# Moving two of the delta rule's four output gate units from the inverses to the input products

## The chip, the cores and the metric

The kernel runs on one core of one Trainium2 chip. The metric is device microseconds of one execution, from the first to the last instruction of the program with what the runtime puts around them. The kernel before takes 2339.52 us, the median of three runs (2337.86, 2339.52 and 2339.65).

## What is computed

A trunk of two layers over 512 latent tokens and 256 context tokens, model width 1024. Each layer mixes the tokens by three groups of heads (gated DeltaNet, latent attention, HGRN2) that share one input and one output projection, and then runs a squared ReLU MLP. The part that matters here, cut from the reference:

```python
def gdn_mixer(pc, px, conv_w, a_log, dt_bias, norm_g, want_ctx):
    # pc, px: columns of h @ w_in for context and latent tokens
    # 0..2: q, k, v (512 columns each)   3: output gate (512 columns)   4, 5: beta and decay
    ...
    def readout(o, gate):
        b, l = gate.shape[:2]
        y = rms_norm(o, norm_g) * jax.nn.silu(gate.astype(F32).reshape(b, l, GDN_HEADS, GDN_DV))
        return y.reshape(b, l, GDN_HEADS * GDN_DV).astype(gate.dtype)
```

Inside `gdn_scan`, each chunk of 64 tokens needs the inverse of a unit lower triangular 64x64 matrix (`triangular_solve` of `eye + lower`). The gate isn't used before the readout, behind the scan. In the last layer the context gets no output, so its gate is not needed.

## The kernel before

**Layout.** Activations lie transposed: 8 blocks of 128 features, 768 tokens along the free axis (256 context, then 512 latent). `lo` is 0 in the first layer and 256 in the second, whose outputs are wanted for latent tokens alone. A unit is 128 output columns of a weight matrix, so `qkv` has 12 units and `gate` 4. A load is 256 columns of weights (1 MB), two units. Loads go through a ring of three slots of the tile `weights`, in the order of the list `LOADS`; SyncE issues a load when the unit that used the slot's last content (`weights_used`) is out. `UNITS` is the order in which units take the four pairs of PSUM banks, and the order of the counter `gemm_evac`.

**Input products.** `qkv` and `ba` units are products in fp32r of high and low parts: ScalarE copies the weights rounded to fp32r (`proj_high_part`, L1747), VectorE subtracts to get the rest (`proj_low_part`, L2300), and TensorE forms high x high, low x high and high x low for each of 8 blocks (`products`, L871, called by `gemm_parts`; `gemm_context_last`, L931, in the second layer). ScalarE then pads each unit (L1894, L1895), VectorE convolves it with five taps (L2430 to L2434) and ScalarE applies Silu (L1902, L1903). Between units 7 and 8 comes a small transpose (`bat`); the decays' chain (L2447 to L2454) follows unit 8 and releases `la_ready`, for which TensorE waits behind unit 9.

**The inverses.** They run over sizes 2, 4, 8, 16 and 32 with two halves `t` of three chunks each. Per size and half TensorE does a first product of 48 small fp32 matmuls (L1180), VectorE masks it (L2534), TensorE does a second product (L1192), and VectorE transposes it (L2550) and adds it to both sides (L2552, L2555), which releases the next size's first product by `u_ready`. The last size (L1177, L1189 to L1195) is handed on by copies of ScalarE (L2015), VectorE (L2546) and GpSimd (L781). GpSimd multiplies decays and attention meanwhile (L770 to L776), once a broadcast of the decays has come back from memory. Behind the last size, products of constants keep TensorE at work (L849), then the corners follow.

**The gates.** The four gate units are spread over the inverses as plain fp32 products, one block of 128 features at a time (`gate_products`: L1151 for 256 context columns, first layer alone, L1152 for 512 latent ones). `gate_work(p)` issues the steps of slot `p` behind each product, by the hand-written table `step_ends`; the first entry is done ahead of the first size. All four units use the same banks 6 and 7, so a unit's first step waits for ScalarE to have emptied the unit before (`hold_gate`, L2000 and L2001), which applies Silu and sends the gate to memory; it comes back much later. Each gate buffer is a half of `state` (`gate_stage`).

## Time and profile before

| | |
|---|---|
| median of 3 runs | 2339.52 us (2337.86 to 2339.65) |
| the profiled execution | 2341.05 us, span 2339.0 us |
| mean granted TensorE clock | 0.988 |
| TensorE busy | 2251.5 us, 96% of the span |
| VectorE, ScalarE, GpSimd busy | 1186.0, 872.9 and 226.6 us |
| input products of the delta rule, first layer | about 58 to 170 us |
| its inverses, first layer | 214 to 294 us |
| input products, second layer | about 1355 to 1458 us |
| its inverses, second layer | 1490 to 1560 us |

Times within the execution are microseconds from the start of the span. PE is TensorE, DVE VectorE, ACT ScalarE, POOL GpSimd and SP SyncE. Rows of the chain of waits give start, length and the piece of work; a plain fp32 matmul of the program appears there as two records (x2), an fp32r one as one. Rows of the timeline merge equal neighbours (xN), so the first start and the length of the merged row count; the shape is that of the first record. A row's length includes the drain, so the spacing of starts tells the rate.

### The profile page before, as it was taken

Reading aid. Unit: us, or ns where it says so; the run is one execution under the profiler, and the core shown is the slowest. Engines: PE = TensorE matmul, PEld = TensorE weight load, DVE = VectorE, ACT = ScalarE, POOL = GpSimd, SP = SyncE. Lnnn points to the kernel's source line nnn. Section 1 sums busy time; section 2 is a strip of 40 time slices with the busy share of each in tenths; the row PEclk is TensorE's granted clock in tenths of the full one; section 3 lists DMA queues with packets and bytes.
Section 4 is the critical chain, followed back from the end, with each engine's and each line's share of the span. In section 5 each row is a group of like instructions: output and inputs, shape, how many; then the busy total and the mean of one; then the engine's idle time right before and its main releaser. Section 6 shows DMA issues by size and latency. Waiting matters only on the chain.

```text
span 2339.0 us, 40119 instructions
## 1 busy us (share of the span) xinstructions
PE 2251.5 (96%) x17754; PEld 1833.2 (78%) x17754; DVE 1186.0 (51%) x1886; ACT 872.9 (37%) x1276; POOL 226.6 (10%) x226
## 2 busy tenths in 40 slices
PE   7999999999999999999999999999998999999998
PEld 5876698876668788888888687668885669888887
DVE  3685353287363651424333497546258556444444
ACT  5363134125463421212123546332324555232233
POOL 3013410000030100000000021511000121000000
PEclk9999999999999999999999999999998999999999
DMA  9218101134211121212121131411116301333222
GB/s 320 63 55 277 45 19 60 54 110 142 87 34 37 37 90 55 72 55 72 55 73 54 54 117 51 135 52 37 54 55 213 119 19 55 108 96 102 90 90 72
DMA packets 161684, 198.27 MB, mean 85 GB/s; under 512 B 18359, under 2 KB 129433, under 8 KB 160872
## 3 DMA queue, kind: packets, MB, share of 16 engines
q1 hardware_dynamic: 155536, 185.24, 24.3%
q10 hardware_dynamic: 5271, 10.10, 1.3%
q8 instruction: 140, 2.29, 0.4%
q0 software_dynamic: 704, 0.37, 0.2%
q14 instruction: 33, 0.26, 0.0%
HBM read 184.64 MB, written 11.06 MB: 84 GB/s over the span
## 4 chain that ended last, share of the span: by engine, by line
PE 86%; DVE 6%; ACT 4%; issue 2%; DMA 1%; POOL 0%; DVEq 0%; ACTq 0%
PE ps L1625 35%; PE ps L871 14%; PE ps L1543 5%; PE ps L1152 3%; PE ps L1021 2%; PE ps L962 2%; PE ps L1478 2%; PE ps L1582 2%; PE ps L1297 1%; PE ps L1315 1%; PE ps L858 1%; PE ps L1180 1%; PE ps L1491 1%; DVE region L2432 1%; PE ps L1192 1%
## 5 line engine op out<-in xcount | busy, mean ns | idle before, releaser
L1625 PE MATMUL ps<-region_r 128*128 128x512 f32 (+1 forms) x1536 | 376.8, 354 | 0.0
L1625 PEld LDWEIGHTS ps<-region_r 128*128 128x128 f32 x1536 | 270.3, 188 | 40.8
L1625 PE MATMUL ps<-region_r,weights_r 128*128 128x512 f32 (+1 forms) x768 | 229.6, 353 | 0.0
L2293 DVE TENSOR_TENSOR weights_r<-weights,region_r 128x2048 fp32r<-128x2048 f32 x62 | 141.9, 2289 | 119.1 <-ACT region_r L1761 119.0
L1625 PE MATMUL ps<-mixed_r,weights_r 128*128 128x512 f32 (+1 forms) x672 | 200.9, 353 | 0.0
L1625 PE MATMUL ps<-modulated_r,region_r 128*128 128x256 f32 (+1 forms) x624 | 186.7, 354 | 0.0
L1625 PE MATMUL ps<-mixed_r,region_r 128*128 128x256 f32 (+1 forms) x624 | 186.6, 353 | 0.0
L2222 ACT ACTIVATE region<-ps,cst 128x768 f32<-128x768 f32 (+1 forms) x64 | 50.4, 798 | 301.2 <-PE ps L1625 282.9
L1625 PEld LDWEIGHTS ps<-region_r,weights_r 128*128 128x128 f32 x768 | 144.3, 188 | 20.5
L2821 DVE TENSOR_TENSOR region_r<-region 128x768 fp32r<-128x768 f32 (+1 forms) x64 | 52.8, 825 | 202.2 <-ACT region L2222 202.2
L1625 PEld LDWEIGHTS ps<-mixed_r,weights_r 128*128 128x128 f32 x672 | 126.3, 188 | 18.1
L1625 PEld LDWEIGHTS ps<-modulated_r,region_r 128*128 128x128 f32 x624 | 117.2, 188 | 16.6
L1625 PEld LDWEIGHTS ps<-mixed_r,region_r 128*128 128x128 f32 x624 | 117.3, 188 | 16.5
L1761 ACT ACTIVATE region_r<-weights 128x2048 fp32r<-128x2048 f32 x62 | 118.4, 1910 | 10.6 <-DMA weights<-in_w_mlp 10.6
L871 PE MATMUL ps<-residual_r,weights_r 128*128 128x512 f32 (+1 forms) x432 | 117.4, 344 | 0.0
L2228 ACT ACTIVATE region<-ps 128x768 f32<-128x768 f32 (+1 forms) x48 | 33.9, 707 | 216.3 <-PE ps L1625 216.3
L2828 DVE TENSOR_TENSOR region<-region 128x768 f32<-128x768 f32 (+1 forms) x32 | 26.4, 826 | 138.9 <-ACT region L2228 138.9
L871 PEld LDWEIGHTS ps<-residual_r,weights_r 128*128 128x128 f32 x432 | 81.1, 188 | 10.6 <-issue 0.2
L739 POOL CAST region_r<-modulated 128x768 fp32r<-128x768 f32 (+2 forms) x24 | 26.1, 1130 | 583.8 <-ACT modulated L1830 546.7
L2300 DVE TENSOR_TENSOR weights_r<-weights,state_r 128x2048 fp32r<-128x2048 f32 x14 | 32.1, 2292 | 84.4 <-ACT state_r L1747 84.4
L1152 PE MATMUL ps<-modulated,weights 128*128 128x512 f32 x128 | 68.9, 636 | 5.2 <-issue 4.4
L871 PE MATMUL ps<-region_r,weights_r 128*128 128x256 f32 (+1 forms) x288 | 73.4, 337 | 0.0
(460 smaller groups left out, 4882.8 us busy)
## 6 DMA issues: line engine op xcount, KB each, us to landing
weights<-in_w_mlp SPq DMA_DIRECT2D x64, 1024.0 KB, 5.3
weights<-in_w_ada SPq DMA_DIRECT2D x40, 1024.0 KB, 5.3
weights<-in_w_in SPq DMA_DIRECT2D x34, 1024.0 KB, 5.3
region<-in_w_ada SPq DMA_DIRECT2D x8, 1024.0 KB, 16.6
weights<-in_w_out SPq DMA_DIRECT2D x8, 1024.0 KB, 6.6
x_kept<-residual SPq DMA_DIRECT2D x2, 3072.0 KB, 12.4
region<-decays_kept ACTq DMA_DIRECT2D x4, 1536.0 KB, 11.0
residual<-x_kept SPq DMA_DIRECT2D x2, 3072.0 KB, 9.9
```

The source lines that it names most:

```text
L871: last = mm(dst[:, CTX + a:CTX + b], w[:, k, m], r[k][:, a:b], start=(k == 0 and w is high and r is r_high), stop=(k == KB - 1 and r is r_ ...
L962: last = mm(dst[:, CTX + a:CTX + b], mat, sq[:, a:b], start=(k == 0), stop=(k == n - 1))
L1021: last = mm(ps[32 * k:32 * k + 32, bank, :], cs[:, 4 * half + k, :], w[:, k, :], start=(half == 0), stop=(half == 1))
L1152: last = mm(ps[:, 6, :], w, Hm[:, k, CTX:TOK], start=(k == 0), stop=(k == KB - 1))
L1478: last = mm(dst[:, CTX + s0:CTX + s1], QH[0:96, h, 128 * qt:128 * qt + 128], KH[0:96, h, s0:s1], start=True, stop=True)
L1543: last = mm(dst[:, at:at + b - a], w[:, k, m], r[:, a:b], start=(k == 0 and part_of == "low"), stop=(k == 5 and w is low))
L1582: last = mm(o, w[:, k, m], r[:, k, a:b], start=(k == 0 and r is Hm_r), stop=(k == KB - 1 and w is low))
L1625: last = mm(dst[:, CTX + a:CTX + b], w[:, k, m], r[:, a:b], start=(k == 0 and r is r_low), stop=(k == KB - 1 and w is low))
L1761: af(mlp_high(j), ring[:, n % NSLOT, :], ACT.Copy).then_inc(w_high_ready, 1)
L2222: copied(l, what, u, af(hid[:, b, lo:], src, ACT.Relu, bias=zero_col))
L2293: v.tensor_tensor(ring_r[:, at, :], ring[:, at, :], mlp_high(j), ALU.subtract).then_inc(w_low_ready, 1)
L2821: v.tensor_tensor(hid_high[:, b, lo:], z, z, ALU.mult)
```

## The change

Units 0 and 1 of the gate leave the inverses. They become fp32r products of high and low parts like `qkv`'s, computed between `bat` and `qkv` unit 8 (`early_gates`). Their weights' load moves from behind the `ada` loads to between `qkv` 3 and `qkv` 4; ScalarE makes the high part in `region` area 5 (`early_gate_high`) and VectorE the low part in the ring. ScalarE's and VectorE's parts of `qkv` 4 and 5 are made later than before. Their Silu goes to block 7 of `residual`, one after the other, and from there to memory (`hold_early_gate`); GpSimd waits for these stores before it clears `residual`. Units 2 and 3 stay as they are, with `step_ends` about halved.

```diff
-    LOADS += [(_l, "qkv", _i) for _i in range(3)] + [(_l, "ba", 0)] + [(_l, "qkv", _i) for _i in range(3, 6)]
+    LOADS += [(_l, "qkv", _i) for _i in range(3)] + [(_l, "ba", 0), (_l, "qkv", 3), (_l, "gate", 0), (_l, "qkv", 4), (_l, "qkv", 5)]
     LOADS += [(_l, "ada", ADA_GDN_AT[_l] + _i) for _i in range(2 * ADA_GDN[_l])]
-    LOADS += [(_l, "gate", _i) for _i in range(2)] + [(_l, "hq", _i) for _i in range(2)] + [(_l, "hf", _i) for _i in range(4)]
+    LOADS += [(_l, "gate", 1)] + [(_l, "hq", _i) for _i in range(2)] + [(_l, "hf", _i) for _i in range(4)]
...
-UNITS = ([("norm0", 0)] + [("qkv", i) for i in range(6)] + [("ba", 0), ("qkv", 6), ("qkv", 7), ("bat", 0), ("qkv", 8), ("qkv", 9), ("gcum", 0)]
+UNITS = ([("norm0", 0)] + [("qkv", i) for i in range(6)] + [("ba", 0), ("qkv", 6), ("qkv", 7), ("bat", 0), ("gate", 0), ("gate", 1), ("qkv", 8), ("qkv", 9), ("gcum", 0)]
...
-         + [("gate", i) for i in range(4)] + [("hq", i) for i in range(4)] + [("grms", i) for i in range(4)]
+         + [("gate", i) for i in range(2, 4)] + [("hq", i) for i in range(4)] + [("grms", i) for i in range(4)]
...
+        def early_weights():
+
+            return R_r[:, 5, 0:2048]
+
         def gate_stage(u):
 
+            if u < 2:
+                return X[:, 7, :]
             return Sf[:, TOK * (u % 2):TOK * (u % 2 + 1)]
...
                 nc.gpsimd.memset(INV64.rearrange("p c h d -> p (c h d)"), 0.0).then_inc(zeros_ready, 1)
+                for kept_sem in gates_kept:
+                    pool.wait_ge(kept_sem, 32 * l + 16)
                 nc.gpsimd.memset(Xf, 0.0).then_inc(zeros_ready, 1)
...
+            def early_gates(l, lo):
+
+                pe.wait_ge(gate_low_ready, LANDED + l + 1)
+                high, low = (z.rearrange("p (k n) -> p k n", k=KB) for z in (early_weights(), ring_r[:, slot(l, "gate", 0), :]))
+                for u in range(2):
+                    dst = free_pair(l, "gate", u)
+                    for k in range(KB):
+                        last = products(dst, high, low, k, slice(128 * u, 128 * u + 128), q_high, q_low, lo)
+                    last.then_inc(gemm_out, 1)
...
                 last.then_inc(gemm_out, 1)
+                early_gates(l, lo)
                 gemm_parts(l, "qkv", 4, [8, 9], q_high, q_low)
...
-                    if k == 0 and u:
+                    if k == 0 and u > 2:
                         pe.wait_ge(gemm_evac, number(UNITS, l, "gate", u - 1) + 1)
...
-                gate_steps = [(u, k) for u in range(4) for k in range(KB)]
-                step_ends = [2, 4, 6, 8, 10] + [10 + 14 * p // 12 for p in range(1, 13)] + [27, 30, 32, 32]
+                gate_steps = [(u, k) for u in range(2, 4) for k in range(KB)]
+                step_ends = [1, 2, 3, 4, 5] + [5 + 7 * p // 12 for p in range(1, 13)] + [13, 15, 16, 16]
...
+                def early_gate_high():
+
+                    n = LOADS.index((l, "gate", 0))
+                    act.wait_ge(w_in_s[n % NSLOT], landed(n))
+                    act.wait_ge(*weights_used(LOADS.index((l, "qkv", 2))))
+                    af(early_weights(), ring[:, n % NSLOT, :], ACT.Copy).then_inc(gate_high_ready, 1)
+
+                def hold_early_gate(u):
+
+                    src = tokens(finished(l, "gate", u), lo)
+                    if u:
+                        act.wait_ge(gates_kept[0], 32 * l + 16)
+                    copied(l, "gate", u, af(gate_stage(u)[:, lo:], src, ACT.Silu, bias=zero_col))
+                    act.wait_ge(gemm_evac, number(UNITS, l, "gate", u) + 1)
+                    act.dma_start(gates_held[l][:, u, lo:], gate_stage(u)[:, lo:]).then_inc(gates_kept[u], 16)
                 for u in range(8):
                     padded(u)
-                    if u % 2 == 1 and (l == 0 or u > 1):
-                        proj_high_part(l, (2, 3, 4, 6)[u // 2])
+                    if u in (1, 3, 5) and (l == 0 or u > 1):
+                        proj_high_part(l, (2, 3, 4)[u // 2])
                     if u:
                         silu(u - 1)
                     if u == 5:
                         copied(l, "ba", 0, af(rows_held, tokens(finished(l, "ba")), ACT.Copy))
+                        early_gate_high()
+                    if u == 6:
                         proj_high_part(l, 5)
                 copied(l, "bat", 0, af(ba[:, :, :], finished(l, "bat")[:, 512:608].rearrange("p (c n) -> p c n", c=NC), ACT.Copy))
                 silu(7)
+                hold_early_gate(0)
+                proj_high_part(l, 6)
+                hold_early_gate(1)
                 padded(8)
...
-                for u in range(3):
-                    hold_gate(u)
+                hold_gate(2)
...
-                    if u in (1, 3, 5, 6, 7) and (l == 0 or u > 1):
-                        proj_low_part(l, {1: 2, 3: 3, 5: 4, 6: 5, 7: 6}[u])
+                    if u in (1, 3, 5, 7) and (l == 0 or u > 1):
+                        proj_low_part(l, {1: 2, 3: 3, 5: 4, 7: 5}[u])
+                    if u == 6:
+                        at = slot(l, "gate", 0)
+                        dve.wait_ge(gate_high_ready, LANDED + l + 1)
+                        v.tensor_tensor(ring_r[:, at, :], ring[:, at, :], early_weights(), ALU.subtract).then_inc(gate_low_ready, 1)
                     convolve(u)
+                proj_low_part(l, 6)
```

## Rows read from the trace of the kernel before

**Rows 1.** The page: TensorE's busy time, and the chain's shares by engine.
```profile
PE   2251.5 (96%) x17754; PEld 1833.2 (78%) x17754; DVE 1186.0 (51%) x1886; ACT 872.9 (37%) x1276; POOL 226.6 (10%) x226
...
PE 86%; DVE 6%; ACT 4%; issue 2%; DMA 1%; POOL 0%; DVEq 0%; ACTq 0%
```

**Rows 2.** Busy time by stage: length, each engine's busy time, granted clock, DMA.
```profile
98.00:142.00 44.00, 43.89 (x254) 37.96 (x252) 26.63 (x28) 19.74 (x32) 0.00 (x0) 1.00 0.23 72
214.00:294.00 80.00, 77.10 (x1402) 52.02 (x1404) 28.41 (x43) 14.48 (x25) 34.50 (x28) 1.00 0.30 96
1486.00:1490.00 4.00, 0.09 (x1) 0.00 (x1) 3.92 (x11) 2.09 (x4) 0.00 (x0) 0.94 0.01 2
1486.00:1500.00 14.00, 9.62 (x57) 4.99 (x57) 5.21 (x14) 4.49 (x7) 0.00 (x0) 0.63 0.64 184
```

**Rows 3.** Chain of waits in the first layer's inverses: start, length, piece.
```profile
215.81 0.43 PE ps L1151 x2
216.24 0.86 PE ps L1152 x2
217.10 1.52 PE ps L1180 x48
218.62 0.63 PE ps L1151 x2
```

**Rows 4.** Who waited: total us, times, longest.
```profile
PE ps L1151 <- ACT state L2001: 1.4, 2, 1.1
...
PE ps L1152 <- ACT state L2001: 0.8, 1, 0.8
```

**Rows 5.** Timeline of TensorE, second layer's inverses: start, length, work.
```profile
1490.47 3.75 PE L1152 MATMUL ps<-modulated,weights 128*128 128x512 f32 x4 [4.38 <-issue]
```

**Rows 6.** Chain of waits in the second layer's inverses: a slot with one step.
```profile
1514.64 1.05 PE ps L1152 x2
```

**Rows 7.** Timeline of TensorE, input products of both layers: first and last rows.
```profile
124.66 0.61 PE L871 MATMUL ps<-region_r 128*128 128x256 f32 x2
...
141.36 0.52 PE L871 MATMUL ps<-mixed_r,region_r 128*128 128x256 f32 x2
...
1368.79 0.47 PE L931 MATMUL ps<-region_r 128*128 128x512 f32 x1
...
1374.32 0.28 PE L931 MATMUL ps<-region_r 128*128 128x256 f32 x1
```

**Rows 8.** Timeline of VectorE, first layer's front stage: `qkv` 4's low part.
```profile
110.20 2.29 DVE L2300 TENSOR_TENSOR weights_r<-weights,region_r 128x2048 fp32r<-128x2048 f32 x1 [1.21 <-ACT region_r L1747]
```

**Rows 9.** The inverses: VectorE's masks as a group, adds, last size.
```profile
L2534 DVE TENSOR_TENSOR mixed<-ps,masks 128x768 f32<-128x768 f32 x8 | 7.7, 958 | 18.7 <-PE ps L1180 18.7
...
227.26 0.58 DVE L2550 STREAM_TRANSPOSE mixed<-ps 128x384 f32<-128x384 f32 x1 [3.34 <-PE ps L1192]
...
228.21 1.19 DVE L2555 TENSOR_TENSOR mixed<-mixed 128x384 f32<-128x384 f32 x1
...
260.54 0.54 DVE L2555 TENSOR_TENSOR mixed<-mixed 128x384 f32<-128x384 f32 x1
...
1509.63 1.64 DVE L2555 TENSOR_TENSOR mixed<-mixed 128x384 f32<-128x384 f32 x1
...
274.27 1.02 PE L1177 MATMUL ps<-mixed,region 32*32 32x32 f32 x96
```

**Rows 10.** Timeline of GpSimd in the first layer's inverses: first product, longest, spread.
```profile
227.71 1.27 POOL L770 TENSOR_TENSOR region<-region 128x512 f32<-128x512 f32 x1 [31.53 <-DMA region<-decays_kept]
...
246.54 1.58 POOL L775 TENSOR_TENSOR region<-region,k_f_sb 128x512 f32<-128x512 f32 x1
...
273.17 3.54 POOL L781 COPY residual<-mixed 32x768 f32<-32x768 f32 x4 [13.22 <-DVE mixed L2555]
```

**Rows 11.** Timeline behind the last size: ScalarE's second spread, TensorE's clock-holding products.
```profile
290.38 2.00 ACT L2015 ACTIVATE residual<-ps 32x384 f32<-32x384 f32 x4 [0.40 <-PE ps L1195]
...
291.40 1.98 PE L849 MATMUL ps<-k_f_sb 128*128 128x512 f32 x4 [1.22 <-DVE mixed L2546]
```

More of the change, by code:

```diff
@@ L356, in trunk_program @@
         LANDED = 16
-        LANDED = 16
-        blocks_ready = ada_in[5]
+        blocks_ready, gate_high_ready, gate_low_ready = ada_in[5:8]
         part_out, part_evac = sem("part_out"), sem("part_evac")
@@ L1993, in hold_gate @@
                 def hold_gate(u):
-                    if u >= 2:
-                        act.wait_ge(gates_kept[u % 2], 32 * l + 16)
                     held = gate_stage(u)
```

## The prediction

> **What bounds the kernel now.** I read the page first: TensorE is busy for 2251.5 of 2339.0 us and the chain that ended last lies on it for 86% [rows 1]. Other engines are half idle, so a change counts by what it does to TensorE's own line, or by a wait that it puts into it. The profiled execution took 2341.05 us around its 2339.0 us span; the median of the three runs is 2339.52, 1.5 less. I sum against 2341.05 and take off 1.5 at the end.
>
> Next I read the two places that the edit touches. The table by stage [rows 2] shows the front stage of the first layer (98 to 142 us) with TensorE busy for 43.9 of 44 us, and the inverses (214 to 294 us) for 77.1 of 80 us, both at full granted clock. In the second layer the inverses start after an idle stretch, and the granted clock is 0.63 over 1486 to 1500: part of it at 1.2 GHz, the rest at 2.4. So both ends of the move are on TensorE's line. What decides is whether the gate steps of the inverses only fill time that TensorE would have spent waiting for VectorE. The chain of waits says no: in the inverses it runs from one TensorE piece to the next, gate steps included, with no VectorE piece between [rows 3].
>
> **What comes out of the inverses.** A gate step of the first layer is one 256 column and one 512 column product in plain fp32, two records each. In the chain a step inside a slot takes 0.43 + 0.86 = 1.29 us; the first step behind an inverse product has 0.63 in place of 0.43, so entering a slot costs 0.20 [rows 3]. Sixteen steps leave: 16 x 1.29 = 20.6 us. By `step_ends` 20 slots held work before (the one ahead of the sizes, and 19), and 15 will: 5 x 0.20 = 1.0 us. TensorE also waited 1.4 us, twice, for ScalarE to empty the gate's bank at a unit's end [rows 4]. One boundary is left, between units 2 and 3; its steps lie on two sides of a 1.52 us inverse product, which covers the evacuation (the longer of those waits was 1.1 us). So 1.4 goes too: 23.0 us.
>
> In the second layer a step has the 512 columns alone, 0.86 us: 16 x 0.86 = 13.8 us. A slot with one step takes 1.05 us, so again 0.19 to enter one and 1.0 for five [rows 6]. The ScalarE wait there is 0.8 [rows 4]. Sum 15.6 us. The start of this stage runs at the lower level: two steps take 3.75 us where they would take 1.72 [rows 5]. I leave the low stretch as long as it is, some 9 us (0.63 over 14 us is 10 us at half rate, under one of them idle), since it follows a 4.4 us idle [rows 5] that the edit doesn't touch (TensorE waits there for VectorE's last pieces, before any gate).
>
> **What the front stage gets.** Two units per layer as three fp32r products. First layer: per block three products of 768 columns. Units 8 and 9, of the same count and with high part and activations both in `region_r` as the new ones have, run from 124.66 to about 141.85: 17.2 us for two [rows 7], or 1.07 a block. Second layer: early gates take the 512 latent columns alone; 24 such products run from 1368.79 to 1374.32, 5.53 us a unit, 11.1 for two [rows 7].
>
> **What else is added, and its cover.** ScalarE copies the high part and VectorE takes the low part, 2.29 us [rows 8]. They stand in the queues where the parts of `qkv` 4 stood; those move one unit back, and those of `qkv` 5 behind unit 7. In the first layer the early low part is then ready at about 112.5 us and wanted at 124.7; `qkv` 4's low part follows unit 6's convolution, near 124, and is wanted at 141.9; `qkv` 5's follows the first early Silu, near 139, and is wanted after 160. In the second layer, where the two early units last 11 us, the narrowest of the three is the early part itself, ready at 1402 and wanted at 1412. So no added wait, cost 0; if the cover were gone, a copy and a subtraction would show, 4.2 us a layer. The decays' chain hangs on unit 8's end, as before, and no longer queues behind unit 7's Silu: 0.1 us to the good, which I leave out. The two Silus, each with its wait for `gemm_evac` and its DMA issue, lie on ScalarE while TensorE works on. The second Silu waits for the first unit's store; queued behind it is unit 8's padding, wanted 8 us later, and VectorE's convolution behind that. No DMA is added: two stores move forward, past nothing else on ScalarE's queue. GpSimd's wait before clearing `residual` is for stores 50 us old. The loads: `gate` 0 takes the slot and the time that `qkv` 4 had on SyncE's queue; `qkv` 4 follows the `ba` unit, `qkv` 5 unit 7, each with a unit or more of slack; the count of loads in the inverses is the same, `hq` 1 in place of a gate. Nothing is added there.
>
> **What becomes late in the inverses.** Per size TensorE has four products of 1.52 us and VectorE two masks of 0.96, then twice transpose, add, add: 0.95 us to the start of the last add, and that takes 0.54 us, but 1.19 to 1.64 while GpSimd works [rows 9]. I wrote both orders out by hand with these numbers. Before, this gives the last size at 274.2 us (traced: 274.3) [rows 9]. After, a handover (0.12 to VectorE, 0.95, the last add, some 0.06 back) of 2.4 us at a last add of 1.25 is covered by a product and one step (3.0 us in the first layer, 2.6 in the second), except where one transposed result queues behind another: 0.05 us and 0.5 us. With every last add beside GpSimd at 1.64 it is 0.8 and 1.7 us. The Trainium skill ("SBUF — State Buffer", Who interferes with whom) has VectorE's instructions with two SBUF inputs blocked for the whole of a GpSimd instruction that reads SBUF. By that rule the trace agrees in kind, with 1.19 us beside 0.54; a full GpSimd instruction of 1.58 us on each add would make the new waits 2.1 and 3.6 us and the forecast 5.1 us later, 2334.9, which is rival (b) below.
>
> GpSimd works from 227.7 to 260.0 and then had 13.2 us to spare [rows 10]. Its start hangs on a DMA, not on TensorE, and the last size now comes near 256.5 us, so its spreading starts 3 us after it could; the corners want it at 270, it ends at 263.5. In the tail of the last size ScalarE must now do the fourth gate's Silu between its two spreads: before, the second spread ran from 290.38 to 292.38 beside products that hold the clock until 293.4 [rows 11], with 1.0 us to spare; by the hand-written order 0.6 us is left in the first layer and 0.5 in the second. Cost 0, and some tenths if the cover is gone.
>
> **The sum.** First layer 23.0 - 17.2 - 0.1 = 5.7 us less. Second layer 15.6 - 11.1 - 0.5 = 4.0 us less. Together 9.7: 2341.05 - 9.7 = 2331.35, less 1.5: **2329.8 us**. Bounds: 0.6 to the good without the new waits (0.1 and 0.5), 2.0 to the bad if slots don't save their entry, 1.9 if the last adds take 1.64: 2329.2 to 2333.7.
>
> **Rivals.** (a) The low clock of the second layer doesn't come, or is shorter. The granted clock was still 0.94 over 1486 to 1490, so it fell only at the very end of that idle stretch [rows 2]; the stage arrives at another moment now. Without it some 9 us at half rate give back up to 4.6: 2325.2. (b) VectorE's chain beside GpSimd costs more than I sum: half the gain goes when each of the eight sizes of both layers loses 0.6 us: 2334.6. For it: TensorE has one step of cover per handover where it had two, and in the first layer six of eight last adds will lie beside GpSimd. Against: per size VectorE works 5 to 7 us and TensorE 8.2 to 8.7. (c) The slower side: the gate steps were cover and the inverses don't shrink. What I take out ahead of the last size is 17.7 us in the first layer (274.2 to 256.5) and 11.8 in the second; if VectorE's handovers bound there, it would come back as waits while the front stages still grow by 28.3: up to 2329.8 + 29.5 = 2359.3. From 1.2 us a size over eight sizes the gain is gone, from 1.8 us it is slower by over 0.2%. Against it stands [rows 3], and VectorE idle for 18.7 us before its masks [rows 9]. (d) The early products don't fit where they are put: TensorE waits for the early part by a copy and a subtraction, 4.2 us a layer: 2338.2, no difference. And if the move itself did nothing, with slots and waits as they were, only the form of the product would be left: 1.29 against 1.07 and 0.86 against 0.69 a step, 6.2 us over 32 steps, 2333.3; that lies within my range.
>
> **How the numbers follow.** My forecast 0.64; (a) 0.12; (b) 0.13; (c) 0.04; (d) 0.07. The range takes in (a) and (b): 2324.0 to 2336.5. About 0.2% (4.7 us) is what a measurement of this kernel can tell from no change, so faster means below 2334.8. The forecast and (a), and half of (b), lie below it, with small parts of the forecast above: 0.80. Same: 0.15. Slower: 0.05.
>
> **What the profile would show.** The early products: 96 fp32r records in the first layer and 48 in the second, 17.2 and 11.1 us, no idle before them nor before `qkv` 4. The inverses: from their first gate step to the clock-holding products 54 us in place of 77.1, GpSimd's spread waiting little. PE idle there under 1 us in the first layer and 2 in the second. If TensorE waits for the last add of VectorE after each size, (b) or (c) is right; if the granted clock over the second layer's start is 1.0, (a). I would be wrong by the fill argument if the inverses shrank by less than 17 us in the first layer.

## The result: slower by 25 us, and the profile after

The changed kernel takes 2364.75 us (median of 4 runs, 2363.33 to 2368.63) against 2339.59 us before (4 runs, 2337.86 to 2341.54): 1.0108 times, 95% interval 1.0092 to 1.0124. I had forecast 2329.8. The profiled execution took 2368.63 us with a span of 2366.4 us, 27.6 above the profiled one before. The program's lines move: TensorE's by 7 (the products are L878, the clock-holding ones L856) or by 18 (gate steps L1169 and L1170, inverse products L1198 and L1210), VectorE's in the inverses by 40 (masks L2574, adds L2595).

The page's row of TensorE shows 25.2 us more busy time with almost the same number of instructions as in [rows 1]: it isn't waiting more, it works more slowly.
```profile
PE 2276.7 (96%) x17802; PEld 1863.8 (79%) x17802; DVE 1190.9 (50%) x1888; ACT 875.1 (37%) x1276; POOL 227.0 (10%) x226
```

To see where, I put the starts of the same lines of code side by side and take the distances, in us. (First layer by a line's first instruction, second layer by its last; for the state update, the first one that reads `region` alone. The last three columns are runs from further on.)

| stretch | before | after | e1 | e5 | e13 |
|---|---|---|---|---|---|
| start to `bat`'s transposition, first layer | 124.2 | 122.7 | 122.3 | 124.0 | 122.7 |
| to the first inverse product | 92.8 | 109.5 | 109.8 | 112.1 | 108.3 |
| to the first corner product | 76.3 | 54.7 | 57.2 | 76.3 | 55.7 |
| to the first diagonal of HGRN | 185.5 | 186.8 | 187.3 | 185.5 | 185.8 |
| to its first state update (levels of HGRN) | 93.7 | 100.2 | 96.4 | 94.2 | 95.5 |
| to `bat`'s last transposition, second layer | 839.7 | 841.4 | 840.7 | 841.4 | 840.7 |
| to the last of the delta rule's first products | 71.0 | 81.4 | 81.5 | 81.5 | 81.5 |
| to the last corner product (inverses) | 82.7 | 97.1 | 65.1 | 80.6 | 62.8 |
| to the last MLP product | 759.2 | 758.3 | 761.4 | 759.2 | 759.9 |

The first layer did what was forecast: 16.7 us more ahead of the inverses, 21.6 less in them. The second layer's front grew by 10.4 us. But its inverses, which were to lose 15.1 us, took 14.4 more. The table of busy time by stage says why (length; busy time and instructions of TensorE, its weight loads, VectorE, ScalarE, GpSimd; granted clock; DMA share and GB/s), to be read against [rows 2]:
```profile
229.00:289.00 60.00, 56.68 (x1344) 40.98 (x1345) 31.73 (x45) 12.83 (x22) 35.95 (x28) 0.97 0.31 102
1490.00:1500.00 10.00, 9.54 (x87) 9.45 (x85) 9.73 (x26) 6.31 (x15) 4.84 (x1) 1.00 0.03 8
1505.00:1570.00 65.00, 65.00 (x792) 47.32 (x790) 20.33 (x32) 2.79 (x4) 20.97 (x16) 0.50 0.17 54
1575.00:1580.00 5.00, 4.68 (x183) 2.54 (x183) 3.77 (x7) 1.13 (x3) 0.00 (x0) 1.00 0.03 7
```
For 65 us TensorE is busy for all of the time and its granted clock is 0.50, that is 1.2 GHz. In the kernel before, the same stage came back to 1.00 at 1500, about 10 us after its first gate step, and stayed there:
```profile
1485.00:1500.00 15.00, 10.62 (x67) 5.99 (x65) 6.17 (x18) 4.49 (x7) 0.00 (x0) 0.66 0.59 172
1500.00:1570.00 70.00, 68.00 (x1480) 45.42 (x1480) 32.08 (x53) 17.95 (x34) 24.46 (x20) 1.00 0.18 56
```
What a slot costs at either level is in the timeline of TensorE. Changed kernel, the start of the second layer's inverses (start, length, work, idle time before it):
```profile
1503.93 2.04 PE L1170 MATMUL ps<-modulated,weights 128*128 128x512 f32 x2 [4.39 <-issue]
1505.90 2.77 PE L1198 MATMUL ps<-mixed,residual 64*64 64x32 f32 x48
1508.61 2.07 PE L1170 MATMUL ps<-modulated,weights 128*128 128x512 f32 x2
1510.61 2.77 PE L1198 MATMUL ps<-mixed,residual 64*64 64x32 f32 x48
```
A slot of one gate step and 48 small products takes 1510.61 - 1505.90 = 4.71 us. With the clock held (run e1 below, whose column stands in the table above) it is 2.58 us, from 1503.44 to 1506.02:
```profile
1497.89 4.54 PE L856 MATMUL ps<-k_f_sb 128*128 128x512 f32 x10
1502.41 1.10 PE L1172 MATMUL ps<-modulated,weights 128*128 128x512 f32 x2
1503.44 1.59 PE L1200 MATMUL ps<-mixed,residual 64*64 64x32 f32 x48
1504.96 1.13 PE L1172 MATMUL ps<-modulated,weights 128*128 128x512 f32 x2
1506.02 1.59 PE L1200 MATMUL ps<-mixed,residual 64*64 64x32 f32 x48
```
At 2.1 us a slot, the 14 or so slots of these 65 us lose 30 us. The granted clock gives the same: 1 less the clock, summed over pieces of 5 us, is 35.8 us from 1500 to 1575 here and 5.1 us from 1485 to 1500 in the kernel before, so 30.7 more. That is the size of the surprise (97.1 where I had 82.7 - 15.1 = 67.6, so 29.5).

### The profile page after: what moved, and what is told of

Read it like the earlier page. It is cut to its first block, busy times and chain, and to the rows that moved or that the text cites. A ratio compares the mean times of both kernels' runs of the same rounds, so it can differ in the third digit from the quotient of the medians.

```text
span 2366.4 us, 40217 instructions
## 1 busy us (share of the span) xinstructions
PE 2276.7 (96%) x17802; PEld 1863.8 (79%) x17802; DVE 1190.9 (50%) x1888; ACT 875.1 (37%) x1276; POOL 227.0 (10%) x226
## 4 chain that ended last, share of the span: by engine, by line
PE 67%; DVE 5%; ACT 3%; issue 2%; DMA 0%; DVEq 0%; POOL 0%; ACTq 0%
PE ps L1643 35%; PE ps L878 8%; PE ps L1561 5%; PE ps L1600 2%; PE ps L1496 2%; PE ps L1170 1%; PE ps L865 1%; PE ps L1509 1%; PE ps L1038 1%; PE ps L856 1%; PE ps L1535 1%; PE ps L1210 1%; PE ps L1198 1%; PE ps L1439 1%; PE ps L1315 1%
## 5 line engine op out<-in xcount | busy, mean ns | idle before, releaser
L1643 PE MATMUL ps<-region_r 128*128 128x512 f32 (+1 forms) x1536 | 376.7, 354 | 0.0
L1643 PEld LDWEIGHTS ps<-region_r,weights_r 128*128 128x128 f32 x768 | 144.3, 188 | 20.6
L1643 PEld LDWEIGHTS ps<-mixed_r,region_r 128*128 128x128 f32 x624 | 117.3, 188 | 16.6
L878 PE MATMUL ps<-residual_r,weights_r 128*128 128x512 f32 (+1 forms) x432 | 117.4, 344 | 0.0
L878 PEld LDWEIGHTS ps<-residual_r,weights_r 128*128 128x128 f32 x432 | 81.1, 188 | 10.6 <-issue 0.2
L878 PE MATMUL ps<-region_r,weights_r 128*128 128x256 f32 (+1 forms) x336 | 87.9, 339 | 0.0
L878 PE MATMUL ps<-region_r 128*128 128x512 f32 (+1 forms) x312 | 74.3, 343 | 0.0
## 6 DMA issues: line engine op xcount, KB each, us to landing
region<-in_w_ada SPq DMA_DIRECT2D x8, 1024.0 KB, 16.6
```

What stands on the lines that cost most here:

```text
L878: last = mm(dst[:, CTX + a:CTX + b], w[:, k, m], r[k][:, a:b], start=(k == 0 and w is high and r is r_high), stop=(k == KB - 1 and r is r_ ...
L1643: last = mm(dst[:, CTX + a:CTX + b], w[:, k, m], r[:, a:b], start=(k == 0 and r is r_low), stop=(k == KB - 1 and w is low))
```

## Experiments

**My theory**: the inverses of the second layer start after 4.4 us in which TensorE idles, and the clock falls there in both kernels. With two gate steps in each of the first slots it rises again after some 10 us; with one step it doesn't rise until the small products of the sizes are over. **R1**: VectorE's handovers now bound the inverses (my own rival (c)), and the low clock goes with TensorE's waits. **R2**: the stage only arrives at another moment, and the front part, not the density, decides. (The texts on the expectations call the first layer L0 and the second L1.)

**e1, the clock held across the gap.** In the changed kernel, behind the last modulation columns:
```diff
                 ada_finish(first + 2 * ADA_GDN[l] - 2, first)
+                if l:
+                    hold_clock(ps[:, 6, :], 5)
```


> The changed kernel with one addition: in the second layer, ahead of the wait that precedes the inverses' first gate step, TensorE multiplies constants (five plain fp32 products of 512 columns, about 4.3 us) where it stood idle for 4.4 us. Theory T (the second layer's inverses of the changed kernel lose about 29 us because they start at the lower granted clock and, with one gate step a slot, never raise it): the clock stays at the upper level from 1504 on, the inverses shrink from about 85 us to about 51, and the kernel comes to 2330 to 2336 us. Rival R1 (VectorE's handovers bound the inverses once the gate steps are gone): no change by holds, 2364 us. Rival R2 (the time shift of the stage alone made the low stretch long): the clock falls somewhere else in the stage, 2350 or more.

Measured: 2333.75 us (median of 12, 2331.14 to 2338.66), 0.9976 times before (0.9967 to 0.9985). The five products fill the idle time almost exactly (4.54 us, rows above), the clock stays at 1.00, and the inverses take 65.1 us in place of 97.1. Nothing in VectorE's work or in the slots was touched, so R1 falls: at the full clock VectorE's chain fits.
```profile
1500.00:1510.00 10.00, 10.00 (x156) 6.02 (x154) 4.11 (x12) 4.15 (x7) 0.00 (x0) 1.00 0.46 173
1510.00:1520.00 10.00, 9.75 (x217) 7.25 (x214) 5.00 (x9) 0.00 (x0) 4.78 (x4) 1.00 0.39 147
1520.00:1530.00 10.00, 10.00 (x236) 7.60 (x234) 7.52 (x11) 0.69 (x1) 9.61 (x9) 1.00 0.09 29
```

**e2, the same in the kernel before.** The same three lines in the kernel before.

> The kernel before with the same five products of constants in the second layer's idle stretch. Theory T: only the 9 us stretch at the lower clock goes, 4 to 5 us less: 2335. R1 and R2: within 1 us of before or the same 4 to 5.

Measured: 2338.62 us, 0.9998 (0.9988 to 1.0008): no difference where I had expected 4 us. The inverses took 80.2 us in place of 82.7 in the profile, so holding the clock is worth 2.5 us there, though a short low stretch from 1555 to 1565 us, which the one before had not, lost 1.7 us in the same stage; this execution had another at 210 us, and run to run the gain is lost among such stretches. Between e1 and this run, the clock held in both, the move itself gains 4.9 us (2333.75 for 2338.62), about half of the 9.7 of my sum. The same edit is worth 31 us in the changed kernel and nothing in this one: what differs is whether the clock comes back by itself.

**e3, a dense start.** The changed kernel, no holding products; only the table of the second layer puts two steps into each of the first slots, and so leaves one in four slots later on:
```diff
                 step_ends = [1, 2, 3, 4, 5] + [5 + 7 * p // 12 for p in range(1, 13)] + [13, 15, 16, 16]
+                if l:
+                    step_ends = [2, 4, 6, 8, 10] + [10 + 3 * p // 12 for p in range(1, 13)] + [14, 15, 16, 16]
```


> The changed kernel with the second layer's sixteen gate steps dealt out otherwise: the first five slots get two steps each, as in the kernel before, the later ones one in four. No work is added or taken away, and the idle stretch stays. Theory T: the clock rises after about 9 us, as in the kernel before; if it then stays, the kernel gets faster by 20 to 29 us (2336 to 2345 us, some of it lost to handovers that are no longer covered); if the sparse rest lets it fall again, by less. R1: sparser later slots cost up to 1 us a handover, 2364 to 2372. R2: as the changed kernel, 2364.

Measured: 2337.22 us, 0.9989 (0.9979 to 1.0000). The same sixteen steps in the same stage, none added, take 27.5 us less in this order:
```profile
1501.31 3.75 PE L1170 MATMUL ps<-modulated,weights 128*128 128x512 f32 x4 [4.39 <-issue]
1504.99 2.77 PE L1200 MATMUL ps<-mixed,residual 64*64 64x32 f32 x48
1507.69 3.26 PE L1170 MATMUL ps<-modulated,weights 128*128 128x512 f32 x4
1510.88 1.59 PE L1200 MATMUL ps<-mixed,residual 64*64 64x32 f32 x48
1512.40 1.98 PE L1170 MATMUL ps<-modulated,weights 128*128 128x512 f32 x4
```
The first piece is, to the hundredth, that of [rows 5]: 3.75 us for two steps. Four records take 3.26 us in the second slot, so the clock rises within it, and the 48 small products go from 2.77 to 1.59 us. From 1515 on the granted clock is 1.00 through slots that hold one step in four.

**e4, the kernel before made sparse.** Its gate units keep the first, third, fifth and eighth of their blocks and leave the others out (half of the gate's products is missing, so the gate is not the reference's); the table is that of the changed kernel. No front part, no other edit:
```diff
-                gate_steps = [(u, k) for u in range(4) for k in range(KB)]
-                step_ends = [2, 4, 6, 8, 10] + [10 + 14 * p // 12 for p in range(1, 13)] + [27, 30, 32, 32]
+                gate_steps = [(u, k) for u in range(4) for k in (0, 2, 4, 7)]
+                step_ends = [1, 2, 3, 4, 5] + [5 + 7 * p // 12 for p in range(1, 13)] + [13, 15, 16, 16]
```


> The kernel before, with half of the gate work of the inverses left out (of eight blocks of every gate unit four are not multiplied) and the changed kernel's table of slots, nothing added elsewhere; the front stage is that of before. So this is the one half of the change alone. By the sum of the prediction it would be 23.0 and 15.1 us faster: 2301. Theory T: the first layer's inverses shrink by about 21.5 us and the second layer's grow by about 14, since the clock stays low: 2330 to 2335. R2: the stage isn't shifted much before the second layer, so the clock would rise as before: 2301 to 2310. R1: both layers shrink little and the clock is at the upper level.

Measured: 2340.99 us, 1.0007 (0.9993 to 1.0020). In the second layer, leaving out half of the gate makes the inverses 14 us longer (96.8 us for 82.7); the first layer's got shorter by about as much. By instructions alone it would have saved 38 us. The time is 6 us above the upper end that my theory gave, since the first layer's inverses were to shrink by 21.5 us and shrank by 14.0 in the profile: there TensorE sat idle for 5.5 us in its last size (266.6 to 272.1 us), for which the view names no cause. That the second layer loses, and where, is as the theory says.
```profile
1480.00:1520.00 40.00, 40.00 (x488) 29.02 (x486) 13.60 (x18) 1.26 (x2) 20.85 (x16) 0.50 0.22 68
1520.00:1560.00 40.00, 37.41 (x786) 24.84 (x786) 13.30 (x24) 8.70 (x15) 3.28 (x4) 0.63 0.24 75
```
There is no early part here and the stage starts where it did before, so R2 falls.

**e5, the early part alone.** The changed kernel with each step of units 2 and 3 issued twice, by the table of the kernel before (`again` keeps the second issue in the same accumulation, so both units come out doubled):
```diff
-                gate_steps = [(u, k) for u in range(2, 4) for k in range(KB)]
-                step_ends = [1, 2, 3, 4, 5] + [5 + 7 * p // 12 for p in range(1, 13)] + [13, 15, 16, 16]
+                gate_steps = [(u, k, again) for u in range(2, 4) for k in range(KB) for again in range(2)]
+                step_ends = [2, 4, 6, 8, 10] + [10 + 14 * p // 12 for p in range(1, 13)] + [27, 30, 32, 32]
```


> The changed kernel with its early part as it is, but with the inverses as dense in gate steps as before: each step of units 2 and 3 is done twice, by the step table of the kernel before (so gate units 2 and 3 come out doubled; that part of the computation is changed, and only the time is read). It measures what the early part costs alone. By my theory (density of TensorE's work in L1's first slots decides the clock): the low stretch of L1 is as short as in the kernel before, about 10 us from the first gate step, L1 from the end of the sixth chunk's first products to the last corner product takes 80 to 84 us (82.7 before, 97.1 after), L0's inverses take 77 us again, and the time is before plus the early part, 16.6 less 1.5 in L0 and 10.5 in L1: 2339.5 + 25.6 = 2365 us, 2360 to 2370, as slow as the changed kernel though it has twice its gate steps in the inverses. If instead the moment at which the inverses start or what ran ahead of them (the early part) sets the clock, L1 keeps 0.50 for 60 us or more and takes over 95 us there: 2378 us or more.

Measured: 2371.36 us (4 runs, 2364.04 to 2373.93), 1.0130 (1.0110 to 1.0149). The median is 1.4 above my range. The table of stretches says where: the second layer is as expected (81.5 and 80.6 us, the low stretch short again, 3.4 us lost), but 2.7 us more lie between the first layer's first products and its inverses, where this execution, unlike the one before, started the inverses at the lower clock. The early part itself costs 16.6 and 10.5 us, as priced. So twice the gate steps in the inverses cost the changed kernel 6.6 us over both layers, where [rows 3] and [rows 6] price them at 20.6 + 13.8.

**e6, one product in the first layer too**: `hold_clock(ps[:, 6, :], (1, 5)[l])` in place of the two lines of e1.

> The changed kernel with five clock-holding products in L1 ahead of the delta rule's inverses, as in the run with them alone, and one such product ahead of L0's inverses too, where the changed kernel's granted clock fell for 5 us after the start. By my theory L1 stays at the full clock and the time is that of the run with L1's alone, 2331 to 2335 us; L0's one product (0.86 us, in 1 us of idle time) moves it by less than 1.5 us either way. By a rival, that the short low stretches of L0 (5 us at 225, 35 to 50 us from 510 on) follow from that idle microsecond, up to 6 us go: 2327 to 2329.

Measured: 2333.63 us (12 runs), 0.9980 (0.9962 to 0.9998): e1's time. In its profile the granted clock is 1.00 from 220 to 240 us, so the first layer's dip is gone; the one in the levels from 510 on is not, so it doesn't follow from the other. One of the twelve runs took 2355.26 us. It has no profile; by its time and its mean clock of 0.977 the second layer's fall may have come there for a part of the stage, which is not shown.

**e9, two products in place of five**: `hold_clock(ps[:, 6, :], 2)` with e1's condition.

> The changed kernel with two clock-holding products in L1 in place of five: 1.7 us of the 4.4 us for which TensorE idles ahead of L1's inverses are filled and 2.7 us stay idle. If the whole idle stretch has to be filled, the clock falls as in the changed kernel and the time is 2355 to 2365 us, with L1 from the end of the first products to the last corner product at 90 us or more. If a part is enough, the time is within 1.5 us of the run with five, 2331 to 2335 us, and that part takes 65 to 68 us. I lean to the second, 6 in 10, since the kernel before idles for 1 to 3 us in other places of L1 at the full clock.

Measured: no single time. Six of twelve runs took 2328.15 to 2339.52 us and six took 2358.39 to 2366.68. The profiled one is of the second group:
```profile
1492.89 1.96 PE L856 MATMUL ps<-k_f_sb 128*128 128x512 f32 x4
1497.42 1.10 PE L1172 MATMUL ps<-modulated,weights 128*128 128x512 f32 x2 [2.56 <-issue]
1498.44 2.23 PE L1200 MATMUL ps<-mixed,residual 64*64 64x32 f32 x48
1500.60 2.07 PE L1172 MATMUL ps<-modulated,weights 128*128 128x512 f32 x2
```
2.56 us stay idle; the first step behind them still runs at the full clock (1.10 us), the second at half (2.07 us). Here the fall comes only after the gap, within the first slot of small products, and by chance: 4.4 us lost it each time in the changed kernel, two products in the gap in half of the runs, by their times. That both of my alternatives came out, 6 to 6, was not foreseen.

**e7, the changed kernel again.**

> The changed kernel once more, unchanged, for a second look at which low stretches of the clock come back. By my theory L1's stretch of 60 to 75 us at 0.50 from its first gate step on comes again at the same place, with 35 to 40 us lost, and the time is 2360 to 2370 us; the short ones elsewhere (225, 510 to 560, 800 to 810, 1785 to 1820) may be longer or shorter by one piece of 5 us each. If L1's stretch is a matter of chance, it is absent or under 30 us here.

Measured: 2364.59 us (one run). The granted clock is below 1 from 1500 to 1570 with 34.1 us lost (1 less the clock, summed over pieces of 5 us), for 35.8 in the first profile. The dip at 225 lasted 15 us here and 10 there, so that one varies.

**e12, wider steps.** The changed kernel's second layer differs from its first in the gate step: 512 columns for 768. This run adds the 256 (and so adds half of each block's columns a second time; gate units 2 and 3 of that layer are changed):
```diff
+                    if l and k:
+                        mm(ps[:, 6, 0:256], w, Hm[:, k, CTX:CTX + 256], start=False, stop=False)
                     last = mm(ps[:, 6, :], w, Hm[:, k, CTX:TOK], start=(k == 0), stop=(k == KB - 1))
```


> The changed kernel with one thing added: in L1 each gate step but the first of a unit has one more product of 256 columns (0.43 us), so that a slot's gate work is as wide as in L0, 768 columns in place of 512, at the same number of steps and places. (It adds half of the unit's columns a second time, so gate units 2 and 3 of L1 are changed, and only the time is read.) In L0 the changed kernel's clock fell for 5 to 15 us after 225 us and came back with one such step in a slot; in L1 it did not come back for 60 to 75 us. My theory, that how much of this work a slot holds decides it: L1's low stretch ends after some 15 to 25 us, 14 x 0.43 = 6 us are added, some 20 to 25 us come back, and the time is 2345 to 2352 us. Rival, that the amount of gate work doesn't matter but the number of steps, or that L1 differs from L0 in something else: the low stretch stays 60 us or longer and the time is 2370 us or more.

Measured: 2346.30 us (10 runs), 1.0024 (1.0011 to 1.0038). More work, 18 us less time than the changed kernel:
```profile
1500.00:1510.00 10.00, 9.85 (x98) 6.63 (x100) 1.00 (x2) 2.40 (x3) 0.00 (x0) 0.50 0.72 272
1510.00:1520.00 10.00, 10.00 (x152) 6.78 (x149) 4.56 (x7) 0.00 (x0) 6.36 (x5) 0.86 0.12 46
1520.00:1530.00 10.00, 10.00 (x248) 8.30 (x245) 6.45 (x9) 0.00 (x0) 9.61 (x8) 1.00 0.02 4
```
With the number of steps, their slots and the gap unchanged, the clock is back by 1515, some 13 us after the first step. So it is what the slots hold, not how many steps there are. It fits that the changed kernel's first layer, whose step is this wide, got away with its dip at 225; nothing was changed in that layer to test it.

**e10, the steps themselves in the gap.** Can useful work hold the clock? In the second layer five steps go ahead of the wait for VectorE's last products (they write bank 6 alone, so they need neither it nor the one for the columns in bank 7). The first layer gets one clock-holding product, as in e6:
```diff
+                if l == 0:
+                    hold_clock(ps[:, 6, :], 1)
...
-                    elif k == 0:
+                    elif k == 0 and lo == 0:
                         pe.wait_ge(ada_read, 2 * l + 1)
...
+                if l:
+                    step_ends = [5, 6, 7, 8, 9] + [9 + 4 * p // 12 for p in range(1, 13)] + [14, 15, 16, 16]
...
-                pe.wait_ge(p1_done, base + NC)
+                if l == 0:
+                    pe.wait_ge(p1_done, base + NC)
                 for u, k in gate_steps[:step_ends[0]]:
                     gate_products(u, k)
+                if l:
+                    pe.wait_ge(p1_done, base + NC)
```


> In place of empty clock-holding products, five of L1's sixteen gate steps themselves run in the 4.4 us for which TensorE idled: they are issued ahead of the wait for the last of VectorE's products (in L1 these steps write bank 6 alone, so they need neither that wait nor the one for the modulation columns in bank 7). The other eleven are spread one in a slot, later fewer. L0 gets one clock-holding product, as in the run with both. My theory: TensorE stays at the full clock in L1, since it never idles and was seen to stay up with one step in four slots; and five steps of 0.86 us leave the slots, so against the run with five empty products 4.3 us go: 2329.5 us, 2327 to 2332. Rival: with fewer steps in the slots the clock falls within the first slots all the same, as in the changed kernel: 2350 or more. Rival: the steps wait for something else there (the gate weights, the columns): 2334 or more.

Measured: 2337.61 us (12 runs, 2329.24 to 2347.11), 0.9992 (0.9976 to 1.0007); 8 us over what I expected. The gap is filled (4.54 us for five steps, no idle) and the start runs at 1.00. Then the thin middle bites:
```profile
1517.98 2.99 PE L1217 MATMUL ps<-mixed 64*64 64x32 f32 x96
1522.09 1.95 PE L1205 MATMUL ps<-mixed,residual 64*64 64x32 f32 x48 [1.13 <-DVE mixed L2602]
1523.98 2.07 PE L1172 MATMUL ps<-modulated,weights 128*128 128x512 f32 x2
```
Two inverse products without a step between them leave VectorE's handover uncovered (1.13 us, the shape of my rival (b)), and right behind it the clock falls; it is 0.76 from 1520 to 1555. It is back for the last size (1.13 us for the step at 1537), so this low stretch too ran to the end of the four smaller sizes. e3 had even fewer steps in the middle but no such wait (TensorE was busy for 38.99 of 39 us from 1505 to 1544 there) and kept its clock. Whether the thinness or the wait tipped it can't be told from these two. The profiled execution (2332.27 us) is among the fastest of twelve that spread over 18 us, so the others may have lost more here; that isn't shown.

**e11, more holds in the HGRN levels.** e10, and `HOLDS_FROM` from `(5, 2)` to `(3, 2)`.

> The same, and in L0's levels of the HGRN stage the kernel's own clock-holding products begin at level 3 in place of level 5 (one more for each of three pair blocks at two levels, six products, 0.70 to 0.86 us each at the full clock). It tests whether the low stretch from 510 us on, 12 to 13.7 us lost in the changed kernel and its variants against 8.5 before, is paid on the path: if so and the products lie in TensorE's idle time (8.4 us of it there), 1 to 4 us go against the run without them, 2325.5 to 2328.5. If the levels wait for VectorE and DMA anyway, nothing goes or up to 5 us come: 2329 to 2335. I lean to the second, 6 in 10: VectorE is busy for 4 us of 5 there.

Measured: 2335.73 us (12 runs), 0.9980 (0.9968 to 0.9993); 1.9 below e10, which is within what either spreads, and 0.7 above the slower of the two ranges that I expected; both started from e10's expected time. In the profiles the low stretch from 510 on lost 5.1 us where e10's lost 6.8, and the levels took 93.2 us against 95.8. A small gain at best.

**e13, a version to beat both.** Three steps and two holding products fill the gap, the middle keeps six steps in place of four, and the rest is as in e11:
```diff
+                hold_clock(ps[:, 6, :], (1, 2)[l])
...
+                if l:
+                    step_ends = [3, 4, 5, 6, 7] + [7 + 6 * p // 12 for p in range(1, 13)] + [14, 15, 16, 16]
```


> A version meant to beat both kernels, from what the runs showed: in L1 three gate steps and two clock-holding products fill TensorE's 4.4 us of idle time (five steps there left the slots so thin that the clock fell from 1520 to 1555 us, 8.6 us lost), the table keeps the next four steps one in a slot and gives the middle slots six in place of four; L0 has one clock-holding product, and its HGRN levels their holds from level 3 on. If the clock is held by these: the run with five empty products (2333.75 us) less 3 x 0.86 = 2.6 us, less 1 to 2 for the levels: 2329 to 2331 us. Rival, that the middle slots are still too thin: the clock falls there once more and the time is 2335 us or more, as with five steps in the gap (2337.6 us).

Measured: 2329.20 us (6 runs, 2328.27 to 2330.43), 0.9962 times before (0.9950 to 0.9975): faster than both kernels, 9.8 us under before and 35.5 under the changed one.
```profile
1490.00:1500.00 10.00, 10.00 (x92) 6.53 (x91) 8.06 (x22) 5.38 (x10) 0.00 (x0) 1.00 0.17 60
1500.00:1510.00 10.00, 10.00 (x232) 7.60 (x232) 4.67 (x8) 0.58 (x1) 0.00 (x0) 1.00 0.67 258
1510.00:1520.00 10.00, 10.00 (x236) 7.60 (x232) 6.42 (x10) 0.69 (x1) 9.01 (x7) 1.00 0.08 30
1520.00:1530.00 10.00, 10.00 (x272) 8.40 (x270) 6.46 (x10) 0.00 (x0) 9.61 (x9) 1.00 0.02 4
```

## Why the prediction was wrong, by its own steps

**The sums held, within 2 us a layer.** The early products cost 16.7 and 10.4 us by the table of stretches, for 17.2 and 11.1. (The first figure also holds the gate steps ahead of the sizes: two before, 2.75 us, and one in the changed kernel, 2.83 us, because it began at the lower clock.) No added copy or subtraction was waited for: in the view of who waited, TensorE has no wait from 105 to 165 us, and from 1395 to 1445 the one of 0.8 us that the kernel before had too; rival (d) is out. In the first layer the inverses ran from 229.4 to the clock-holding products at 285.0, 55.6 us, where I had 54 in place of 77.1; the dip of the clock between 225 and 235 us, 1.7 us lost, accounts for the difference. By the table the inverses came out 21.6 us shorter where I had 22.9, of which the one step ahead of the sizes, 1.3 us, falls into the stretch before. TensorE's waits from 229 to 290 us, forecast under 1 us in the inverses, are
```profile
PE ps L856 <- DVE mixed L2586: 1.2, 1, 1.2
PE ps L1226 <- issue: 1.0, 1, 1.0
PE ps L1213 <- issue: 0.7, 1, 0.7
PE ps L1169 <- issue: 0.5, 1, 0.5
```
of which the first stood before, too [rows 11], the second lies in the corners behind the inverses, and the last ahead of the first gate step; 0.7 us is left. None is behind a mask or an add of the sizes 2 to 16.

**VectorE beside GpSimd** behaved as by the rows: its last adds averaged 1.12 us in the first layer's inverses of the changed kernel, inside my 0.54 to 1.64 of [rows 9], and the sizes' products never waited for them.
```profile
L2595 DVE TENSOR_TENSOR mixed<-mixed 128x384 f32<-128x384 f32 x8 | 8.9, 1116 | 0.0
L2574 DVE TENSOR_TENSOR mixed<-ps,masks 128x768 f32<-128x768 f32 x8 | 7.6, 956 | 10.4 <-PE ps L1198 10.4
```
The idle time before the masks fell from 18.7 us [rows 9] to 10.4, and was still there. So (b) and (c) are out for this kernel; e10 shows (b)'s wait where two products lie with no step between them.

**The step that failed** is one sentence: "I leave the low stretch as long as it is, some 9 us ..., since it follows a 4.4 us idle ... that the edit doesn't touch". The edit doesn't touch the idle time (4.38 us before, 4.39 after), which is why the clock falls. But it takes out half of what the clock came back by. I had read the fall in [rows 2] and [rows 5] and asked only whether it would still happen, as rival (a) shows, never what had ended it. The low stretch is not a fixed length behind a gap; it lasted 7 to 10 us with two steps a slot (before, e3, e5), some 13 with one step and 256 columns more (e12), and to the end of the four smaller sizes with one step of 512 columns (after, e4, e9). The price is 29.5 us in the second layer's inverses; with early products 0.7 us cheaper than forecast it turns the gain of 4.0 that I had for the layer into a loss of 24.8.

**The slower side** had the right picture with the wrong mechanism. Rival (c) said that the gate steps were cover; they were, not for VectorE but for the clock. I gave it 0.04 because both rows that I used to reject it, the chain without VectorE pieces and VectorE's idle time, speak of waits. Neither can speak of a rate.

**The rest.** The time missed the forecast by 35.0 us, and 29.5 of them are this step. With the clock held the kernel takes 2333.75 us. My sum was made with a 9 us low stretch; without one it was 2325.2, so 8.5 us are missing in e1. Its profiled execution was 3.6 us above its median, 2337.4, and 10.7 above a sum of 2326.7 made as that of the profiled one before. By the table these lie in the first layer's front and inverses (2.1 us gained of 5.7, with a dip of the clock from 225 to 240 that the kernel before didn't have: 3.6), in the second layer's (7.1 of 8.6: 1.5), in the HGRN levels (2.7) and in three stages that the edit doesn't touch (1.8, 1.0 and 2.2), less 1.9 at the very start. The levels took 93.7 us before, 100.2 in the changed kernel's profile, 97.7 in e7, and 93.2 to 98.2 in its variants, and the low stretches of the clock there lose from 5 to 14 us. What makes them vary is not shown and stays open; that they are longer in the changed kernel rests on two profiles.

By the Trainium skill ("TensorE: Matmul & The Clock Gate", "Loop structure matters more than you think") matmuls issued back to back, with results copied out beside them, keep the clock up, and long waits between them lose it. As to the loss the trace agrees: the clock falls behind the 4.4 us gap. Of the return the section says nothing; taken for that, too, it would have let the changed kernel, busy for 65.0 of 65.0 us in the rows, come back as soon as the kernel before, at an estimated 2364.75 - 29.5, some 2335 us. The measured 2364.75 us decides.

## What to carry to other kernels

A filler beside small matmuls on TensorE has a second use that no wait shows: before taking work out of a stage, look up whether the stage's clock falls at its start, and what stands in the slots in which it comes back. If it falls, fill the gap that makes it fall, first with work that has to be done anyway, or put the wide products into the first slots; the same sixteen steps cost 27.5 us more or less by their order alone (changed kernel and e3). Don't empty the middle of the stage for it: with five of the sixteen steps in the gap the clock fell there (e10). And a stage that reads 100% busy can still be at half speed, so read the granted clock beside each busy time, and read a version's spread: the best version (e13) also had the narrowest runs (six, within 2.2 us).

## What the runs showed of the hardware

- TensorE busy throughout by its records, and the granted clock 0.50 for 65 us (1505 to 1570, changed kernel; 1480 to 1520 with 40.00 of 40 us busy in e4). No rival of mine held such a stretch.
- At 1.2 GHz the small products are not halved but nearly: 48 of 64 rows and 32 columns took 2.77 us for 1.59, a gate step 2.07 for 1.13 (lengths with the drain; the slot 4.71 for 2.58).
- After a short gap the clock can fall late, and by chance: the first step behind 2.56 us of idle time took 1.10 us, the next 2.07 (e9), and six of that version's 12 runs have the slow time; behind 4.4 us all five of the changed kernel's runs have it; with the gap filled by five products, none of e1's twelve (the longest 2338.66 us), and one of e6's twelve lies between (2355.26 us).
